# The first block of a two-block model on one core: tap columns, key spread, convolution norm and Silu move to other engines and other steps

## The reference

```python
proj = xn @ w_in
q_a, kv_a, k_rope, conv_in = jnp.split(proj, [o1, o2, o3], axis=-1)
q = (rms_norm(q_a, g_q_a) @ w_q_b).reshape(b, s, MLA_HEADS, QK_NOPE_DIM + QK_ROPE_DIM)
kv = (rms_norm(kv_a, g_kv_a) @ w_kv_b).reshape(b, s, MLA_HEADS, QK_NOPE_DIM + V_HEAD_DIM)
q_rope = apply_rope(q_rope, cos, sin)      # per head
k_rope = apply_rope(k_rope, cos, sin)      # one for all heads
attn = causal_mla_attention(q_nope, q_rope, k_nope, k_rope, v)
a, gate = jnp.split(conv_in, 2, axis=-1)
c = a * jax.nn.sigmoid(gate)
c = causal_depthwise_conv(c, conv_w, conv_b)          # 31 taps, 512 channels
c = jax.nn.silu(layer_norm(c, conv_ln_g, conv_ln_b))
return jnp.concatenate([attn, c], axis=-1) @ w_o
```

## Time and profile before

| what | value |
|---|---|
| median of 3 runs | 1173.52 us (1171.37 to 1174.31) |
| the profiled execution's own time | 1172.35 us |
| its span in the trace | 1170.5 us |
| TensorE busy | 1121.0 us, 96% |
| VectorE busy | 787.7 us, 67% |
| ScalarE busy | 621.9 us, 53% |
| GpSimd busy | 351.1 us, 30% |

### The profile page before, as it was taken

One profiled execution on the slowest core, in us unless ns is written; L12 is line 12 of the kernel. 1 busy time (PEld: TensorE's weight loads), 2 busy tenths in 40 slices (PEclk: granted clock), 3 DMA queues, 4 the chain that ended last, 5 costly groups with the idle time before them and its releaser, 6 DMA issues.

```text
span 1170.5 us, 24132 instructions
## 1 busy us (share of the span) xinstructions
PE 1121.0 (96%) x8909; PEld 1066.4 (91%) x8909; DVE 787.7 (67%) x1401; ACT 621.9 (53%) x1191; POOL 351.1 (30%) x380
## 2 busy tenths in 40 slices
PE   6879789999998999999999999999999999999997
PEld 6876779999997978869999999999979999999996
DVE  5774488888467776746788655496556567898454
ACT  5455556655545556665566534474425655666343
POOL 4221042343313101124566412200013334666130
PEclk9899889999999999969999999999999999999998
DMA  6454047766556533303555554565422565555651
GB/s 193 129 157 126 2 144 192 200 183 203 168 172 210 182 109 109 109 2 111 178 179 176 182 169 156 191 209 180 162 72 77 188 203 161 182 183 181 205 184 54
DMA packets 202489, 180.61 MB, mean 154 GB/s; under 512 B 6800, under 2 KB 200755, under 8 KB 202163
## 3 DMA queue, kind: packets, MB, share of 16 engines
q1 hardware_dynamic: 201907, 175.74, 48.0%
q0 software_dynamic: 512, 3.94, 0.9%
HBM read 176.28 MB, written 1.05 MB: 151 GB/s over the span
## 4 chain that ended last, share of the span: by engine, by line
PE 85%; DVE 7%; ACT 3%; issue 2%; POOL 2%; DMA 1%; SPq 0%; ACTq 0%; DVEq 0%; POOLq 0%
PE ps L1864 24%; PE ps L1865 24%; PE ps L1866 24%; PE ps L2222 2%; DVE wlo L1260 2%; PE ps L2352 2%; PE ps L2023 1%; POOL acc L572 1%; ACT whi L760 1%; PE ps L2179 1%; DVE ta L1476 1%; PE ps L2204 1%; PE ps L2330 1%; PE ps L2058 1%; PE ps L2178 1%
## 5 line engine op out<-in xcount | busy, mean ns | idle before, releaser
L1260 DVE TENSOR_TENSOR wlo<-raw,whi 128x1024 fp32r<-128x1024 f32 x321 | 399.8, 1283 | 171.0 <-ACT whi L760 169.7
L760 ACT ACTIVATE whi<-raw 128x1024 fp32r<-128x1024 f32 x322 | 323.8, 1050 | 168.6 <-PE ps L1866 143.8
L1864 PE MATMUL ps<-xh,whi 128*128 128x256 f32 (+1 forms) x912 | 264.7, 290 | 17.6 <-DVE wlo L1276 4.8
L1865 PE MATMUL ps<-xl,whi 128*128 128x256 f32 (+1 forms) x912 | 260.7, 286 | 0.0
L1866 PE MATMUL ps<-xh,wlo 128*128 128x256 f32 (+1 forms) x912 | 260.3, 285 | 0.0
L1864 PE MATMUL ps<-xrh,whi 128*128 128x274 f32 (+2 forms) x832 | 242.0, 291 | 0.0
L1865 PE MATMUL ps<-xrl,whi 128*128 128x274 f32 (+2 forms) x832 | 238.6, 287 | 0.0
L1866 PE MATMUL ps<-xrh,wlo 128*128 128x274 f32 (+2 forms) x832 | 238.5, 287 | 0.0
L1864 PEld LDWEIGHTS ps<-xh,whi 128*128 128x128 f32 x912 | 177.4, 195 | 22.1 <-issue 18.1
L1864 PE MATMUL ps<-fh,whi 128*128 128x256 f32 (+1 forms) x688 | 193.7, 282 | 2.2 <-DVE wlo L1260 2.2
L1866 PE MATMUL ps<-fh,wlo 128*128 128x256 f32 (+1 forms) x688 | 193.7, 281 | 0.0
(11 more groups left out here) (334 smaller groups left out, 1567.0 us busy)
## 6 DMA issues: line engine op xcount, KB each, us to landing
raw<-ffn_w SPq DMA_DIRECT2D x128, 512.0 KB, 4.4
raw<-ret_w_in SPq DMA_DIRECT2D x48, 512.0 KB, 4.4
raw<-even_w_in SPq DMA_DIRECT2D x24, 512.0 KB, 4.6
raw<-w_ffn_gate SPq DMA_DIRECT2D x22, 512.0 KB, 4.0
raw<-w_ffn_up SPq DMA_DIRECT2D x22, 512.0 KB, 5.2
raw<-w_ffn_down SPq DMA_DIRECT2D x16, 512.0 KB, 4.5
raw<-ret_w_out SPq DMA_DIRECT2D x16, 512.0 KB, 4.4
raw<-w_in SPq DMA_DIRECT2D x12, 512.0 KB, 5.5
```

The costliest lines, as they stand in the source:

```text
L760: A(whi[:, slot, s * 1024:s * 1024 + 1024], raw[:, slot, s * 1024:s * 1024 + 1024], ACT.Copy).then_inc(w_hi_ready, 1)
L1260: V.tensor_tensor(wlo[:, slot, s * 1024:s * 1024 + 1024], raw[:, slot, s * 1024:s * 1024 + 1024], f32(whi[:, slot, s * 1024:s * 1024 + 102 ...
L1864: T.matmul(dst, w[0], x[0], start=first, stop=False)
L1865: T.matmul(dst, w[0], x[1], start=False, stop=False)
```

## The change

- The tap columns are built by VectorE: block 0 behind the last convolution input, blocks 1 to 3 behind the query rotation. GpSimd no longer takes part.
- The key is rotated by one more VectorE instruction and spread over the heads by one ScalarE copy.
- SyncE issues 8 of the first 16 shifted copies between the two query loads, and all 32 before the first output load.
- The weights of output chunks 0 and 1 are both split inside the head loop (steps 2 to 9). Before, chunk 0 was split ahead of it.
- Three taps stand in each of steps 0 to 7, none later. The convolution sums stand in step 9.
- The mean is taken away by GpSimd, which also makes the low halves of the convolution part. VectorE multiplies by gain and inverse deviation in one instruction.
- Silu is made of Exp on ScalarE, then on VectorE one added, a reciprocal of each 128x256 tile, and a product, in steps 14 and 15. The two table loads are gone.
- TensorE makes the convolution part of output chunk 0 in steps 16 to 19, and the small lambda product stands behind chunks 0 and 1.
- Scores and turned tiles change places in PSUM; three semaphores are merged into others.

```diff
-        SCORES = (4, 5)
+        SCORES, TURNED = (0, 1), (4, 5)
...
-        TAPS_BEFORE, TAPS_BESIDE = 8, 2
-        CSTAT_AT = 14
+        TAPS_BEFORE, TAPS_BESIDE = 8, 3
+        CSTAT_AT = 9
...
+        MIX_AT = 16
...
-            return max(0, TS * (m + 1) - TAPS_BEFORE) // TAPS_BESIDE
+            return -(-max(0, TS * (m + 1) - TAPS_BEFORE) // TAPS_BESIDE)
...
             for j in range(2):
                 c = C0["q"] + j
                 columns(c, c % 2, a["w_q_b"][0], 3, 4 * QHEAD * j, 4 * QHEAD)
+                if j == 0:
+                    shifted(0, (0, 1))
...
-            shifted(0)
+            shifted(0, (2, 3))
+            shifted(1, range(TG))
             c = C0["mix_out"]
...
-            for j in range(1, 4):
+            for j in range(4):
                 columns(c + j, (c + j) % 2, a["w_o"][0], KD, 256 * j)
...
-            pool.wait_ge(const_in, 32)
-            pool.wait_ge(cols_ready, 3)
-            pool.wait_ge(pt_done, 1)
-            taps_of = [P, TG * TS, 32]
-            for m in range(CT):
-                nc.gpsimd.tensor_tensor(diag[m], eye[:, :].unsqueeze(1).broadcast_to(taps_of),
-                                        cw[:, TG * TS * m:TG * TS * (m + 1)].unsqueeze(2).broadcast_to(taps_of), ALU.mult).then_inc(diag_ready, 1)
             for m in range(CT):
                 pool.wait_ge(g_sig, m + 1)
                 nc.gpsimd.tensor_tensor(conv_in[:, m, TAPS - 1:TAPS - 1 + N1], ta[:, m % 2, 0:N1], ra[:, m % 2, 0:N1], ALU.mult)\
                     .then_inc(conv_in_ready, 1)
...
-            heads = [P - NOPE, HEADS, N1]
-            pool.wait_ge(conv_in_ready, CT)
-            pool.wait_ge(krope_mul, 1)
-            nc.gpsimd.tensor_tensor(kt_[NOPE:P, :, :], rope_t[NOPE:P, 0, :].unsqueeze(1).broadcast_to(heads),
-                                    rope_t[NOPE:P, 1, :].unsqueeze(1).broadcast_to(heads), ALU.add).then_inc(krope_ready, 1)
-            pool.wait_ge(krope_ready, 1)
...
+            pool.wait_ge(cmu_ready, 1)
+            for m in range(CT):
+                nc.gpsimd.tensor_tensor(cv[:, m, :], cv[:, m, :], mu[:, 0:N1], ALU.subtract).then_inc(c_mid, 1)
+            for m in range(CT):
+                pool.wait_ge(c_hi, m + 1)
+                nc.gpsimd.tensor_tensor(x1l[:, 4 + m, :], sq6[:, m, :], f32(x1h[:, 4 + m, :]), ALU.subtract).then_inc(c_ready, 1)
...
                 A(qt[0:NOPE, 2 * j:2 * j + 2, :], both("q", j)[0:NOPE], ACT.Copy).then_inc(q_ready, 1)
+                if j == 0:
+                    act.wait_ge(krope_mul, 1)
+                    A(kt_[NOPE:P, :, :], rope_t[NOPE:P, 0, :].unsqueeze(1).broadcast_to([P - NOPE, HEADS, N1]), ACT.Copy).then_inc(krope_ready, 1)
...
-                if j == 0:
-                    split_at(C0["q"] + 3)
...
+                if i in (2, 4, 6, 8):
+                    split_at(C0["mix_out"] + (i - 2) // 4, ((i // 2 - 1) % 2,))
...
+                if i == CSTAT_AT + 3:
...
-                if i == 17:
-                    nc.scalar.preload_act_table(ACT.Silu)
+                if i in (CSTAT_AT + 4, CSTAT_AT + 5):
+                    for m in ((0, 1), (2, 3))[i - CSTAT_AT - 4]:
+                        act.wait_ge(cn_ready, m + 1)
+                        A(sq6[:, m, :], cv[:, m, :], ACT.Exp, bias=low_b[:, m:m + 1], scale=-1.0).then_inc(c_exp, 1)
+                if i in (CSTAT_AT + 6, CSTAT_AT + 7):
+                    for m in ((0, 1), (2, 3))[i - CSTAT_AT - 6]:
+                        act.wait_ge(silu_ready, m + 1)
+                        A(x1h[:, 4 + m, :], sq6[:, m, :], ACT.Copy).then_inc(c_hi, 1)
...
-            for m in range(CT + 1):
-                if m < CT:
-                    act.wait_ge(cn_ready, m + 1)
-                    A(sq6[:, m, :], cv[:, m, :], ACT.Silu, bias=c2("conv_ln_b", m), scale=c2("conv_ln_g", m)).then_inc(silu_ready, 1)
-                if m >= 1:
-                    act.wait_ge(silu_ready, m)
-                    A(x1h[:, 3 + m, :], sq6[:, m - 1, :], ACT.Copy).then_inc(c_hi, 1)
-            nc.scalar.preload_act_table_set("natural_log_exp_and_others")
...
             link(V.tensor_tensor(rope_t[R, 0, :], qkv[R, 5, :], trig, ALU.mult))
             V.tensor_copy(rope_t[NOPE:QHEAD, 1, :], rope_t[QHEAD:P, 0, :])
-            V.tensor_copy(rope_t[QHEAD:P, 1, :], rope_t[NOPE:QHEAD, 0, :]).then_inc(krope_mul, 1)
+            link(V.tensor_copy(rope_t[QHEAD:P, 1, :], rope_t[NOPE:QHEAD, 0, :]))
+            V.tensor_tensor(rope_t[R, 0, :], rope_t[R, 0, :], rope_t[R, 1, :], ALU.add).then_inc(krope_mul, 1)
...
+            dve.wait_ge(const_in, 32)
+            tap_columns(0)
...
-            split_at(C0["q"] + 3)
+            for m in range(1, CT):
+                tap_columns(m)
+            V.tensor_scalar(low_b[:, :], col2[:, R2AT["conv_ln_b"]:R2AT["conv_ln_b"] + CT], -1.0, None, ALU.mult)
...
+                if i in (3, 5, 7, 9):
+                    split_at(C0["mix_out"] + (i - 3) // 4, ((i // 2 - 1) % 2,))
+                if i == CSTAT_AT + 2:
...
-                    for m in range(CT):
-                        ins = V.tensor_tensor(cv[:, m, :], cv[:, m, :], mu[:, 0:N1], ALU.subtract)
-                    ins.then_inc(dve_chain, 1)
-                    centred = chain.up()
...
                     for m in ((0, 1), (2, 3))[i - CSTAT_AT - 3]:
-                        V.tensor_tensor(cv[:, m, :], cv[:, m, :], musq[:, 0:N1], ALU.mult).then_inc(cn_ready, 1)
+                        dve.wait_ge(c_mid, m + 1)
+                        V.scalar_tensor_tensor(cv[:, m, :], cv[:, m, :], c2("conv_ln_g", m), musq[:, 0:N1], ALU.mult, ALU.mult).then_inc(cn_ready, 1)
+                if i in (CSTAT_AT + 5, CSTAT_AT + 6):
+                    pair = ((0, 1), (2, 3))[i - CSTAT_AT - 5]
+                    for m in pair:
+                        dve.wait_ge(c_exp, m + 1)
+                        ins = V.tensor_scalar(sq6[:, m, :], sq6[:, m, :], 1.0, 3.0e38, ALU.add, ALU.min)
+                    link(ins)
+                    for m in pair:
+                        ins = V.reciprocal(sq6[:, m, :], sq6[:, m, :])
+                    link(ins)
+                    for m in pair:
+                        V.scalar_tensor_tensor(sq6[:, m, :], cv[:, m, :], c2("conv_ln_b", m), sq6[:, m, :], ALU.add, ALU.mult).then_inc(silu_ready, 1)
...
-            for m in range(CT):
-                dve.wait_ge(c_hi, m + 1)
-                V.tensor_tensor(x1l[:, 4 + m, :], sq6[:, m, :], f32(x1h[:, 4 + m, :]), ALU.subtract).then_inc(c_ready, 1)
...
+            def mixed(k):
+                pe.wait_ge(o_ready, 2 + k // 2) if k < 4 else pe.wait_ge(c_ready, k - 3)
+            def mix(j, *tiles, first=False, last=False):
+                c = C0["mix_out"] + j
+                return product(c, c % 2, pair("mix_out", j, N1), rows_x1, TOK1, 256, kt=len(tiles), order=tiles, first=first, last=last, ready=mixed)
...
+                if i >= MIX_AT:
+                    pe.wait_ge(max_ready, 16)
+                    mix(0, 4 + i - MIX_AT, first=i == MIX_AT)
+            pe.wait_ge(o_norm, 16)
+            mix(0, 0, 1)
+            mix(1, 4, 5, 6, 7, first=True)
+            mix(0, 2, 3, last=True).then_inc(mm_done, 1)
+            mix(1, 0, 1, 2, 3, last=True).then_inc(mm_done, 1)
             pe.wait_ge(meta_ready, 1)
             pe.wait_ge(lam_one, 1)
-            pe.wait_ge(max_ready, 16)
+            pe.wait_ge(pT_ready, 16)
             T.matmul(ps[4][:, 0:1], ones[0:1, :], lam_s[:, 4:5], start=True, stop=True).then_inc(lam_done, 1)
             c = C0["mix_out"]
-            for tiles in (range(4), range(4, KD)):
-                for j in range(2):
-                    ins = product(c + j, (c + j) % 2, pair("mix_out", j, N1), rows_x1, TOK1, 256, kt=4, order=tiles,
-                                  first=tiles[0] == 0, last=tiles[0] == 4, ready=mixed)
-                    if tiles[0] == 4:
-                        ins.then_inc(mm_done, 1)
             for j in (2, 3):
                 pe.wait_ge(tile_ready, TILES[S_MIX] + 2 * j - 2)
```

56 lines of the change are left out of this document (23 added, 33 removed).

## The result

| | before | after |
|---|---|---|
| median of 6 runs each | 1174.07 us (1171.37 to 1174.54) | 1180.24 us (1177.96 to 1181.44) |
| the profiled execution's own time | 1172.35 us | 1177.96 us |
| its span | 1170.5 us | 1176.1 us |

The ratio is 1.0054, with an interval of 1.004 to 1.0068: the changed kernel is 5 to 8 us slower. Its profiled execution is the fastest of its six.

What follows compares the result with a forecast made beforehand. TensorE was taken to bound the kernel (85% of the chain of waits). -6.3 + 2.8 + 7.0 + 3.5 + 1.1 = +8.1 on the profiled 1172.35 us gave 1180.45, median 1181.6 us; range 1172.5 to 1186.0.

Steps and rivals of the forecast that it cites:

- A: Chunk 2's weight split: with tap columns off GpSimd, TensorE's wait and slow clock there go; -6.3 us (-7.0 to -5.5).
- B: Query weights: the second query load, issued behind eight tap copies, makes TensorE wait longer; +2.8 us (+1.5 to +4.5).
- C: Head loop: sums come earlier, but VectorE's reciprocals of 2.3 us each lengthen steps 14 and 15; +7.0 us.
- D: Lambda product behind chunks 0 and 1: late first output copy delays chunk 2, +3.5 us; slow clock after it, +1.1.
- rival 1: Head loop: the reciprocal costs as a plain instruction, C is -0.6, total +0.5, 1174.0 us; chance 0.22.
- 2 (load in time): Query weights: the second query load arrives in time, without slow clock, 4.3 us less, 1177.3 us; chance 0.06.
- 3: Head loop steps 12 to 17: GpSimd's eight new 128x256 instructions block VectorE, +2.8, 1184.4 us; chance 0.08.
- 4: Weight loads on shared queues eat A's gain: A only -3, total +11.4, 1184.9 us; chance 0.08.

Runs made afterwards that it cites:

- run 4: Kernel before with only the tap columns built on VectorE in place of GpSimd: 1169.16 us, ratio 0.9956 to before.
- run 1: Changed kernel with the one-column lambda product ahead of chunk 0's first o tiles, not behind chunks 0 and 1: 1177.32 us, ratio 1.0023 to before.
- run 3: Changed kernel with its four 128x256 reciprocals replaced by a product with 1.0, leaving out the Silu's division: 1173.72 us, ratio 0.9995 to before.
- run 11: Changed kernel with the four subtractions of the convolution's mean back on VectorE in place of GpSimd: 1180.79 us, ratio 1.0065 to before.
- run 2: Changed kernel with the second query load issued ahead of the eight tap copies: 1174.29 us, ratio 1.0002 to before.
- run 5: Kernel before with tap columns on VectorE, and the key spread on ScalarE in place of GpSimd: 1168.24 us, ratio 0.9946 to before.
- run 6: Kernel before with the lambda product moved behind chunks 0 and 1: 1176.42 us, ratio 1.0022 to before.
- run 12: Changed kernel with lambda product and second query load moved earlier, and ScalarE's Ln and exp replacing VectorE's sum and reciprocal: 1169.34 us, ratio 0.9951 to before.
- run 7: Changed kernel with the lambda product ahead of chunk 0's o tiles and the second query load ahead of the tap copies: 1171.77 us, ratio 0.9974 to before.
- run 8: Changed kernel with lambda product and second query load moved earlier, and ScalarE's Silu replacing exp, sum, reciprocal and product: 1167.23 us, ratio 0.9947 to before.

## Why the prediction was right, and where its sum was off

The direction was right, and 1180.24 us lies 1.4 from the 1181.6. The mechanisms of A, B and D were right in size too, that of C in kind; how near the total came is in part luck, as the sum below shows. Point by point, with the times of the trace:

- **A: -6.3 predicted, -6.7 in the trace, -5.2 by itself (run 4).** The split, the start near 30 and the clock came as worked out: the low half was to be ready at 29.95, and TensorE starts at 30.00. The next load landed in time for the product of chunk 6 to start at 55.55 (55.5 to 56.5 predicted). In all fourteen traces the sums stand at 48.05 and 50.20 with the tap columns on GpSimd and at 41.0 to 44.6 without. Alone it gives less, as the first tap block then stands in front of the query rotation (run 4).
- **B: +2.8 predicted, +2.8 measured** (6.7 gained, 3.88 left). The wait was put at 7.5 us and is 7.56. That the 2.8 agree so closely is chance: as the distance from the sums to the first scores B is 2.8 to 3.6 us over the executions (43.95 and 44.35 in before's order; 47.17, 47.50, 47.46 and 47.28 in after and runs 1, 3 and 11). The prediction weighed only the query load; `w_kv_b` stands behind the eight copies as well, which run 2 brings out. And the small sum hides two large ones: the load's place costs 6.1 us (run 2), and the key spread's move gives 7 us at the loop's start (run 5) that the loop doesn't keep.
- **C: +7.0 predicted, +3.9 in the trace. This is the term that was mis-sized, and the step of it that failed is the price of the reciprocal.** "Three quarters of its 11 ns as paid per column" gave 2.3 us; it is 1.7. Four of them make 2.4 of the 3.1 us. The rest is in small steps: in times of before the sums came at 114.35 (115.0 predicted), the first product with rstd at 120.1 (121.1). The order of events was right: VectorE sets the pace in steps 14 and 15 and the value products wait behind it. Steps 14 and 15 take 5.18 each and not 6.35.
- **D: +3.5 predicted, +3.4 in the trace; the slow clock behind it +1.1 predicted, +1.6 measured** (the fourth copy of y is 5.05 late, the first 3.43). That is 5.0 from the end of chunks 0 and 1 on. As a whole kernel's cost it is 2.6 us on before (run 6) and 3.6 on after (run 1): the slow clock ahead of these chunks was 1 to 2 us longer or shorter at the same time. The 1.0 us between the two lies within the intervals; whether it is chance or follows from the edit is open.
- **The sum:** -6.7 + 2.8 + 3.9 + 3.4 + 1.6 = +5.0, and 0.6 in later stages make the 5.6 of the spans. Predicted were 8.1, 2.5 too many: C is 3.1 too dear, A 0.4 too small a gain, and D's slow clock and the later stages give back 1.1. The forecast of the time came nearer than this, because the profiled execution of after is the fastest of its six and the ratio gives +6.3: 0.6 us of the 2.5 are made up by which executions were profiled, and another 0.6 by the median of before, which is 1174.1 over six runs and was 1173.5 over three. That part is luck.
- **Rivals.** 1 (a reciprocal at the price of a plain instruction, 0.38) is refuted by the row of 3.37 for two; its threshold of 1.3 us was passed. Had it held, run 3 shows the outcome: 1173.7, and rival 1 said 1174.0. 2 (load in time) is refuted by the issue at 63.16; run 2 made it true by another order, and gave 1174.3 (1177.3 said): the rival had put the price of the late load at 4.3 us, and it is about 6. 3 by run 11 and the reciprocals' length. 4 by the sums at 41.35 and run 4.

The Trainium skill, SBUF — State Buffer, section "SBUF: two separate sides", has VectorE with two SBUF inputs and GpSimd exclude each other for a whole instruction. The trace agrees: run 4 shows 4.70 us beside a GpSimd instruction of 4.53, and 0.35 once it is gone (after). Beside GpSimd's subtractions of 0.7 us each VectorE's pair of products takes 0.6 us longer (1.47 against 0.88, run 11), which fits the same rule.

The Trainium skill, VectorE: DVE Perf Modes, section "Walkthrough: the 8-slice pipeline in each mode", led to the estimate of 2.1 us and start-up for 256 columns. The measured 1.7 us is below it, so the repeat count of 8 isn't the price of a column here.

## What to carry to other kernels

Work that is moved off a blocking engine pays in full only if the order of transfers stays, so look at what each queue issues ahead of the load that is waited for: eight small copies cost 6 us, more than the whole head loop's rearrangement (3.9). A one-column product and its negation cost 2.6 to 3.6 us because the copy of a large tile stood behind them; put such a thing where its consumer engine idles. And a stage that starts 7 us earlier keeps little of it if the work that its old start covered (tap blocks, a weight load) isn't moved as well.

## What the runs showed of the hardware that was not expected

- VectorE's reciprocal over 128x256 float32 takes 1.7 us, 6.6 ns a column, where the neighbours on that tile take about a quarter of it or less (a pair of sums 0.48, a pair of products 0.88). Over one column it looks like any other.
- ScalarE forms the same function as Ln and exp of 512 columns in 1.35 us, 2.5 times as fast as the pair of reciprocals (3.37), without a table load between 81 and 171 us in run 12.
- Far behind the change, from 490 to 540, TensorE is busy all the time (in before and in runs 4, 5 and 7), and its granted clock is 0.76 in before and in run 4 but 0.73 in runs 5 and 7, whose code there is the same. An earlier start alone doesn't set it: run 8 has its first scores as early as run 7 (82.84 and 82.77), and has 0.76. What sets it isn't settled.
- Executions of one kernel differ ahead of any change: in run 3 the first scores come at 92.02 and in after at 88.52, with the same instructions up to there. The clock granted from 20 to 40 was 0.83 in the one and 1.00 in the other, from 60 to 95 it was 0.85 and 0.90. Of the 3.5 us 3.2 are there already at the sums (44.56 and 41.35): TensorE had waited 1.17 us at 21.72 in run 3, and its clock was 0.50 from 24 to 30; after has no such wait and 1.00 there. A stage's cost is better read as a distance within one execution than from absolute times.
